# Gated attention scores counted from the middle of 128-token blocks, with six buffers of scaled keys and queries

## What is computed

```python
gcum = jnp.cumsum(gc, axis=1)                  # per key channel, within the chunk
q_t = qc * jnp.exp(gcum)                       # q was scaled by 128 ** -0.5
k_t = kc * jnp.exp(-gcum)
att = jnp.where(causal, einsum('blhk,bshk->blsh', q_t, k_t), 0.0)
o = einsum(att, vc) + einsum(q_t, state)
state = state * exp(g_end) + einsum(kc * exp(g_end - gcum), vc)
```

## Time and profile before

| | us |
|---|---|
| median of 3 runs | 1341.23 |
| the profiled execution's own time | 1341.43 |
| its span | 1339.6 |
| PE busy | 1320.0 (99%) |
| PE weight loads busy | 1119.0 (84%) |
| DVE busy | 777.4 (58%) |
| ACT busy | 641.8 (48%) |
| POOL busy | 621.8 (46%) |

### The profile page before, as it was taken

The page is one execution under the profiler, slowest core; times in us unless marked ns, Lnnn a source line. Parts: engine busy times, 40 slices in busy tenths (PEclk is TensorE's granted clock), DMA queues, the critical chain, the costliest instruction groups (busy, mean ns, idle before and its releaser), DMA issues.

```text
span 1339.6 us, 16496 instructions
## 1 busy us (share of the span) xinstructions
PE 1320.0 (99%) x6630; PEld 1119.0 (84%) x6630; DVE 777.4 (58%) x890; ACT 641.8 (48%) x1033; POOL 621.8 (46%) x294
## 2 busy tenths in 40 slices
PE   7999999999999999999999999999999999999997
PEld 6878878888898888888889888898998888888887
DVE  5857386840079998885002753386279988882002
ACT  5654787653355444443233576454554544443221
POOL 3344561245424644445553364554535544445551
PEclk9999999999999999999999999999999999999999
DMA  6332111123223332333333223301323333333331
GB/s 206 95 113 85 51 37 40 63 79 98 92 85 103 97 95 94 94 93 100 94 94 103 96 79 95 95 16 63 112 95 95 95 94 98 102 93 88 100 87 63
DMA packets 41452, 119.78 MB, mean 89 GB/s; under 512 B 4384, under 2 KB 12960, under 8 KB 41376
## 3 DMA queue, kind: packets, MB, share of 16 engines
q1 hardware_dynamic: 40160, 116.34, 28.5%
q10 hardware_dynamic: 1216, 2.38, 0.6%
HBM read 116.35 MB, written 2.23 MB: 89 GB/s over the span
## 4 chain that ended last, share of the span: by engine, by line
PE 93%; DVE 4%; ACT 1%; issue 1%; DMA 0%; ACTq 0%; DVEq 0%
PE bank L336 26%; PE bank L337 26%; PE bank L338 26%; PE bank L1774 1%; PE bank L1775 1%; PE bank L1773 1%; PE bank L2077 1%; PE bank L2059 1%; PE bank L1506 1%; PE bank L1509 1%; PE bank L1325 1%; PE bank L387 1%; PE bank L1292 1%; PE bank L1536 1%; DVE sqacc L663 1%
## 5 line engine op out<-in xcount | busy, mean ns | idle before, releaser
L319 POOL TENSOR_TENSOR wlo<-raw,whi 128x1024 fp32r<-128x1024 f32 (+2 forms) x215 | 531.1, 2483 | 633.9 <-ACT whi L313 633.8
L336 PE MATMUL bank<-xw_hi,whi 128*128 128x512 f32 (+1 forms) x1280 | 478.0, 373 | 8.6 <-DVE xw_lo L646 8.1
L338 PE MATMUL bank<-xw_hi,wlo 128*128 128x512 f32 (+1 forms) x1280 | 473.8, 370 | 0.0
L337 PE MATMUL bank<-xw_lo,whi 128*128 128x512 f32 (+1 forms) x1280 | 473.7, 370 | 0.0
L313 ACT ACTIVATE whi<-raw 128x1024 fp32r<-128x1024 f32 (+2 forms) x217 | 221.5, 1025 | 208.0 <-DMA raw<-in_fout 112.2
L336 PEld LDWEIGHTS bank<-xw_hi,whi 128*128 128x128 f32 x1280 | 242.5, 189 | 50.3 <-issue 8.9
L338 PEld LDWEIGHTS bank<-xw_hi,wlo 128*128 128x128 f32 x1280 | 242.3, 189 | 41.1
L337 PEld LDWEIGHTS bank<-xw_lo,whi 128*128 128x128 f32 x1280 | 242.5, 189 | 39.8 <-issue 0.2
L596 DVE RECIPROCAL small<-small 128x2 f32<-128x2 f32 x8 | 1.3, 165 | 315.1 <-ACT small L521 313.7
L715 DVE SCALAR_TENSOR_TENSOR cbuf<-ubuf,par,cbuf 128x510 f32<-128x510 f32 x100 | 168.7, 1687 | 3.5
L711 DVE SCALAR_TENSOR_TENSOR cbuf<-ubuf,par,cbuf 128x510 f32<-128x510 f32 x100 | 144.6, 1446 | 4.7 <-ACT cbuf L844 4.1
(11 more groups left out here) (278 smaller groups left out, 1453.9 us busy)
## 6 DMA issues: line engine op xcount, KB each, us to landing
raw<-in_fin SPq DMA_DIRECT2D x88, 512.0 KB, 3.6
raw<-in_fout SPq DMA_DIRECT2D x32, 448.0 KB, 3.3
raw<-in_gin SPq DMA_DIRECT2D x25, 512.0 KB, 3.6
raw<-in_hin SPq DMA_DIRECT2D x24, 512.0 KB, 3.7
raw<-in_hout SPq DMA_DIRECT2D x16, 512.0 KB, 3.6
raw<-in_fout SPq DMA_DIRECT2D x16, 512.0 KB, 3.6
raw<-in_gout SPq DMA_DIRECT2D x8, 512.0 KB, 3.9
xres<-in_x SPq DMA_DIRECT2D x8, 256.0 KB, 5.8
```

Of the source, the lines that this page charges most:

```text
L319: engine.tensor_tensor(wlo[s][:, 0:n], raw[s][:, 0:n], whi[s][:, 0:n].bitcast(F32), ALU.subtract).then_inc(w_lo, 1)
L336: first = nc.tensor.matmul(out_ap, wh, ah, start=start, stop=False)
L337: nc.tensor.matmul(out_ap, wh, al, start=False, stop=False)
L338: return first, nc.tensor.matmul(out_ap, wl, ah, start=False, stop=stop)
```

## The change

1. After each cumulative sum, DVE moves the origin of the exponents to the middle of each 128-token block: `dve_from_middle(t)` copies the chunk ends to `ends` (128x8) and subtracts them from every second chunk of `gl` (128x256). It is placed in turn t + 1 between `least` and the subtraction; the last one follows turn 7. With that origin one set of keys serves a whole 128-token block.
2. `dve_carries` is one add in place of 2 memsets, 8 copies and 4 adds; `carry` has one column per head, direction and request.
3. `dve_keys` is one 128x512 product in place, of `ek`; `kk`, its memsets and its 3 products by `carry` go. `qx` is `qt` times one column.
4. `scores(n)` has, for each request, three products of 128 columns (two diagonal blocks and one off it) in place of four of 64 and one of 128.
5. There are six buffers of `qt`, `ek` and `qx`. Exponents of n = 0 to 5 come after turn 7 on ACT (those of 4 and 5 behind one `hi`), keys in pairs behind the evictions of turns 9, 10 and 11 on DVE (n = 4, 5 behind the last eviction), queries one per block on POOL from block 19 on.
6. The scale 128 ** -0.5 goes into the exponent of `qt`, as a bias (ln of it). The masks are now unscaled (`up + eye` for the forward direction, `1 - up` for the backward one), and the diagonal is counted twice by the 2 that `up + eye` has on it. For d = 1, `own_scores` is one `copy_predicated` from the bank into `att` per request, in place of a product in the bank and an add.
7. On ACT the loading of the exponent table (through a 1-element `Exp`) comes behind three `cross_scores`; exponents of 4 and 5 are gone from the GLA phase; `outs(0)` is split around `cross_scores(1, 1)`.
8. Some semaphores are merged (`cst_in` and `rope_in`; the three small loads of the GLA layer; the last stores).

```diff
-                    for c in range(NCH):
-                        s = c // 2
-                        nc.tensor.matmul(out[:, s * SEQ + c * CH:s * SEQ + (c + 1) * CH],
-                                         kks(n)[:, r, c * SEQ + s * P:c * SEQ + (s + 1) * P],
-                                         qt[n % 4][:, r * SEQ + c * CH:r * SEQ + (c + 1) * CH], start=True, stop=True)
-                    c, s = (2, 0) if d == 0 else (1, 1)
-                    last = nc.tensor.matmul(out[:, s * SEQ + (1 - s) * P:s * SEQ + (2 - s) * P],
-                                            kks(n)[:, r, c * SEQ + s * P:c * SEQ + (s + 1) * P],
-                                            qx[n % 4][:, r * P:(r + 1) * P], start=True, stop=True)
+                    def against(s, queries, to):
+                        return nc.tensor.matmul(out[:, s * SEQ + to * P:s * SEQ + (to + 1) * P],
+                                                ek[n % AHEAD][:, r * SEQ + s * P:r * SEQ + (s + 1) * P], queries,
+                                                start=True, stop=True)
+                    for s in range(2):
+                        against(s, qt[n % AHEAD][:, r * SEQ + s * P:r * SEQ + (s + 1) * P], s)
+                    last = against(d, of_request(qx[n % AHEAD], r, P), 1 - d)
...
+        def dve_from_middle(dve, t):
+            d = t // GLA_HEADS
+            at, last = slice(t * NREQ * NCH, (t + 1) * NREQ * NCH), 0 if d else CH - 1
+            dve.wait_ge(sem("gate_scan"), t + 1)
+            nc.vector.tensor_copy(ends[:, at].unsqueeze(2), chunks_of(t)[:, :, last:last + 1]).then_inc(
+                sem("gate_ends"), 1)
+            dve.wait_ge(sem("gate_ends"), t + 1)
+            early = chunks_of(t)[:, d::2]
+            nc.vector.tensor_tensor(early, early, ends[:, at][:, d::2].unsqueeze(2).broadcast_to([P, NREQ * NCH // 2, CH]),
+                                    ALU.subtract).then_inc(sem("gate_mid"), 1)
...
+                    if ft:
+                        dve_from_middle(dve, t - 1)
                     dve.wait_ge(sem("gate_act"), 3 * t + 3)
...
+                if t > G0:
+                    for n in (2 * (t - G0) - 2, 2 * (t - G0) - 1):
                         dve_keys(dve, n)
...
+                if at >= BASE["gin"] + 19:
+                    pool_queries(pool, at - BASE["gin"] - 19)
...
+            nc.scalar.activation(qt[n % AHEAD][:], gl[:, f], ACT.Exp, bias=prm("lnqg"), scale=GK_NORM).then_inc(sem("gla_e"), 1)
...
+            nc.vector.tensor_tensor(ek[n % AHEAD][:], ck(gqkv, 4 + n // 2), ek[n % AHEAD][:], ALU.mult).then_inc(
+                sem("gla_kk"), 1)
...
                 if d:
-                    dve.wait_ge(sem("gla_db"), 2 * hd + 2)
                     dve.wait_ge(sem("gla_df"), 2 * hd + 2)
+                    mask = tri[:, P:2 * P].bitcast(mybir.dt.uint32).unsqueeze(1).broadcast_to([P, 2, P])
                     for r in range(NREQ):
-                        nc.vector.tensor_tensor(scores[r], scores[r], other[r], ALU.add).then_inc(sem("gla_dg"), 1)
+                        nc.vector.copy_predicated(own[r], mask, blocks(sbank(d, r)[:])).then_inc(sem("gla_db"), 1)
...
+            cross_scores(0, 0)
+            cross_scores(0, 1)
+            cross_scores(1, 0)
             nc.scalar.activation(small[:, 5:6], prm("eps"), ACT.Exp)
-            cross_scores(0, 0)
-            act_gate_exps(act, 4)
-            cross_scores(0, 1)
-            act_gate_exps(act, 5)
-            cross_scores(1, 0)
             act_gate_exps(act, 6)
-            outs(0)
+            out(0, 0)
             cross_scores(1, 1)
+            out(0, 1)
+            cross_scores(2, 0)
             act_gate_exps(act, 7)
-            cross_scores(2, 0)
             outs(1)
...
             own_scores(0, 0)
             own_scores(0, 1)
-            dve_zero_keys(dve, 3)
-            dve_keys(dve, 3)
             own_scores(1, 0)
-            dve_keys(dve, 4)
-            dve_keys(dve, 5)
+            dve_keys(dve, 6)
             own_scores(1, 1)
             own_scores(2, 0)
-            dve_keys(dve, 6)
             dve_keys(dve, 7)
...
-            for n in (4, 5):
-                pool_queries(pool, n)
             squares(0)
```

More of the change, by code:

```diff
@@ L9 @@
+import math
 from contextlib import ExitStack
@@ L33 @@
 QG = float(P) ** -0.5
+AHEAD = 6
 FF = 2816 // P
@@ L237, in build_program @@
                 tri = sb("tri", 2 * P, F32, q)
[L238 to L241, removed]
+                ek = [sb(f"ek{i}", T, F32, q) for i in range(4)] + [ek4, ek5]
+                qt = [sb(f"qt{i}", T, F32, q) for i in range(4)] + [qt4, qt5]
+                qx += [qx4, qx5]
             with ExitStack() as q:
@@ L1835, in way @@
             return ap[:, ::-1] if d else ap
-        CARRIES = 18
-        def dve_carries(dve):
[L1841 to L1867, removed]
@@ L1869, in dve_gin @@
+        def dve_carries(dve):
+            dve.wait_ge(sem("gate_ends"), G0)
+            by_chunk = ends[:].rearrange("p (i c) -> p i c", c=NCH)
+            nc.vector.tensor_tensor(carry[:].unsqueeze(2), by_chunk[:, :, 1:2], by_chunk[:, :, 2:3], ALU.add).then_inc(
+                sem("carry_set"), 1)
         def dve_gin(dve):
@@ L1995, in dve_keys @@
[L1995 to L2004, removed]
@@ L2219, in own_scores @@
                 dve.wait_ge(sem("gla_s"), 2 * hd + d + 1)
-                mask = tri[:, d * P:(d + 1) * P].unsqueeze(1).broadcast_to([P, 2, P])
-                scores = [blocks(att[hd % 2][:, r * T:(r + 1) * T]) for r in range(NREQ)]
-                other = [blocks(sbank(d, r)[:]) for r in range(NREQ)]
-                for r in range(NREQ):
-                    nc.vector.tensor_tensor((other if d else scores)[r], blocks(sbank(d, r)[:]), mask,
-                                            ALU.mult).then_inc(sem("gla_db" if d else "gla_df"), 1)
+                own = [blocks(of_request(att[hd % 2], r, T)) for r in range(NREQ)]
                 if d:
-                    dve.wait_ge(sem("gla_db"), 2 * hd + 2)
                     dve.wait_ge(sem("gla_df"), 2 * hd + 2)
+                    mask = tri[:, P:2 * P].bitcast(mybir.dt.uint32).unsqueeze(1).broadcast_to([P, 2, P])
                     for r in range(NREQ):
-                        nc.vector.tensor_tensor(scores[r], scores[r], other[r], ALU.add).then_inc(sem("gla_dg"), 1)
+                        nc.vector.copy_predicated(own[r], mask, blocks(sbank(d, r)[:])).then_inc(sem("gla_db"), 1)
+                else:
+                    mask = tri[:, 0:P].unsqueeze(1).broadcast_to([P, 2, P])
+                    for r in range(NREQ):
+                        nc.vector.tensor_tensor(own[r], blocks(sbank(d, r)[:]), mask, ALU.mult).then_inc(sem("gla_df"), 1)
             def reciprocals(hd):
```

155 lines of the change are left out of this document (54 added, 101 removed).

## The result

| | before | after |
|---|---|---|
| median of 4 runs each | 1341.33 | 1355.89 |
| the profiled execution's own time | 1341.43 | 1353.49 |
| its span | 1339.6 | 1351.7 |

The ratio after to before is 1.0106, 95% interval 1.0093 to 1.0119. The forecast was 1337.6 with a range to 1339.8. In the attention the change did what was forecast; PE had become slower ahead of it and behind it.

The account below looks back on a forecast made before the run. The prediction took PE, busy 99% of the span, as the bound. Attention gains of 4.7 us less a 1.1 us wait gave -3.6 on 1341.43, 1337.8, or 1337.6 as a median; range 1334.9 to 1339.8.

Parts of the forecast that it names:

- What costs nothing: Step listing parts priced at zero: later exponents, queries one per block, the bias and dropped scale, merged semaphores.
- PE's price of scores: Scores on PE: six weight loads replace ten at 0.111 us each, 0.445 us less per request, at most 7.1 us.
- V0 to V1: Attention, between PE's loads for the users of attention 0 and 1: 8.51 us becomes 6.35, gain 2.15.
- V1 to V2: Attention, between PE's loads for the users of attention 1 and 2: 11.25 us becomes 8.7, gain 2.55.
- V2 to V3: Attention, between PE's loads for the users of attention 2 and 3: no score in it, 5.4 us as before.
- S0 to V0: Attention's start, from the first scores to their first user on PE: PE waits 3.0 us, gain taken as 0.
- keys of 4 and 5 blocked: At the attention's start, DVE's key products wait behind POOL's instructions; without the blocking 1.9 us would be gained.
- V0 has 0.75 us to spare: First user of the attention on PE: a slower copy_predicated costs nothing there until 0.75 us is used up.
- copy_predicated: DVE's masking in the attention: taken as 0.38 us each, though no row showed this instruction.
- gate(3), +1.1: Input projection, turns 1 and 2: DVE's new product and cumulative sum are blocked by POOL, so PE waits 1.1 us.
- rival A: PE doesn't wait at gate(3), as the product or the sum gets ahead of POOL's `lo`: -4.7, 1336.5 us; chance 0.17.
- The sum without the layout: Whole kernel: -4.7 us in the attention plus 1.1 at gate(3), -3.6 us on 1341.43.

Follow-up runs that it names:

- with 512 bytes: The changed kernel with unused bytes behind the parameter tile, so everything behind stands 512 bytes further than before the change: 1336.49 us, ratio 0.9969.
- mask and add: Kernel after with 512 bytes, backward diagonal blocks masked in the bank and added instead of copy_predicated: 1338.22 us; the same on top of the later keys: 1336.34 us.
- the later keys: Kernel after with 512 bytes, keys of 4 moved behind own_scores(0, 1) and keys of 5 behind own_scores(1, 0): 1333.42 us, ratio 0.9946.
- the kernel after with 64 bytes: The changed kernel with 32 unused bytes behind the parameter tile, so tiles behind it stand 64 bytes further than before the change: 1343.12 us, ratio 1.0018.

## Why the prediction was wrong

Point by point, by its own steps:

- **The failed step** is in "What costs nothing": "The bias and the dropped scale change no instruction's size." The instructions kept their size, but the bias is read from a new column of the table, and that column moved every tile behind it by 32 bytes. The step priced it at nothing, and none of the rivals had it; the runs show 18.0 us (profiled executions of the kernel after with and without 480 bytes more). Without that shift the same change is 4.1 us faster than the kernel before.
- **PE's price of scores, V0 to V1, V1 to V2:** right. Forecast 6.35, 8.7 and 5.4 for V2 to V3; measured 6.42, 8.70, 5.41.
- **S0 to V0, keys of 4 and 5 blocked:** right in place and cause. PE waits 2.58 us (forecast 3.0), and S0 to V0 goes from 7.03 to 6.80, a gain of 0.2 (forecast 0). "V0 has 0.75 us to spare" was too much: with 512 bytes ACT's copies of S1 end at 881.63 and V0 starts at 882.20, 0.5 us to spare. DVE and POOL of the kernel after, which answer to the earlier trace rows (the rows up to 790 us are turn 1 and `least` of turn 2):
```profile
783.78 2.58 DVE L1852 TENSOR_TENSOR gl<-gl,ends 128x256 f32<-128x256 f32 x1
...
787.00 1.22 DVE L1894 TENSOR_TENSOR_SCAN gl<-gmask,ubuf 128x512 f32<-128x512 f32 x1
...
789.32 0.74 DVE L1876 TENSOR_SCALAR ubuf<-bank,par 128x512 f32<-128x512 f32 x1
...
888.88 3.17 DVE L1947 TENSOR_TENSOR ek<-gqkv,ek 128x512 f32<-128x512 f32 x2
...
892.81 0.77 DVE L2156 COPY_PREDICATED att<-tri,bank 128x256 f32<-128x256 uint32 x2
```
```profile
780.55 5.53 POOL L316 TENSOR_TENSOR wlo<-raw,whi 128x1024 fp32r<-128x1024 f32 x2 [9.25 <-ACT whi L310]
787.01 3.43 POOL L316 TENSOR_TENSOR wlo<-raw,whi 128x1024 fp32r<-128x1024 f32 x1 [0.93 <-ACT whi L310]
...
887.46 2.37 POOL L316 TENSOR_TENSOR wlo<-raw,whi 128x1024 fp32r<-128x1024 f32 x1 [1.20 <-ACT whi L310]
...
891.58 0.94 POOL L1962 TENSOR_TENSOR qx<-qt,carry 128x256 f32<-128x256 f32 x1
```
- **`copy_predicated`:** right, 0.77 for two, 0.38 to 0.39 each. That is why mask and add cost 0.76 per loop in the runs above. Whether POOL holds it up, the rows above don't show: POOL's product ends at 892.52, and it starts at 892.81. With the later keys the two overlap, and neither is longer for it:
```profile
878.74 0.78 DVE L2157 COPY_PREDICATED att<-tri,bank 128x256 f32<-128x256 uint32 x2 [0.51 <-PE bank L1990]
...
878.90 0.61 POOL L1963 TENSOR_TENSOR qx<-qt,carry 128x256 f32<-128x256 f32 x1
```
- **gate(3), +1.1:** did not come; on this point rival A held. The product was blocked as forecast (2.58 in place of 0.43 in the next turn), but the cumulative sum starts at 787.00 and POOL's `lo` at 787.01: the sum is first, takes 1.22 and not 3.3, and it is the `lo` that becomes long (3.43). `least` ends at 790.06 and gate(3) goes at 791.76 with no wait, as the products around it. The kernel after with 512 bytes has the same order (777.42 and 777.43), so the step doesn't hang on the slower pace. A margin forecast at -0.4 us came out at +0.01: the blocked product ended 0.28 us behind the `lo` that held it (786.08 to 786.36; 0.5 was assumed), and the subtraction started at 786.29, 0.07 ahead of the product's end, where 0.1 behind it was assumed.
- **The sum without the layout:** -4.7 + 1.1 was forecast, -4.87 measured in the attention. On the 1341.43 of the profile that gives 1336.6; the kernel with 512 bytes has a median of 1336.49. That is rival A's 1336.5 and not the forecast's 1337.6, though inside the range.
- **A term that was missing:** after a wait of PE of 2.6 us the clock can fall, below.

## What to carry to other kernels

An edit that adds a few bytes to a tile moves every tile behind it: before costing a change, compare where the operands of the hot loop lie, and here keep the distance of matmul's moving operand and its weights modulo 256 bytes. Where PE is busy all the time, count its instructions in a window of fixed length; the busy share hid 5 products in 135. When a change loses where none of its instructions stand, first make the old kernel with the new layout and nothing else: one run showed that no instruction of the change was to blame.

## What the runs showed of the hardware

**The distance of PE's two operands.** A product of 128x512 follows the one before after 0.2267 us, or after 0.2333 if the addresses of the activations and the weights differ from the free distance by 32 bytes; 256 and 512 are free, and a shift of both by 32 is free. It is so whichever of the two moves: in the value products of the input projection (L1769 to L1771 of the kernel after) the activations are loaded as weights and the blocks in the slots are the moving operand, and the pace is 0.233 after and 0.227 before. The Trainium skill's page "SBUF — State Buffer", section "Who interferes with whom", says that PE reads the moving operand and the weights through two ports that are independent, and that PE never waits on anyone. In this case's traces neither port has to wait for another engine as far as a row shows, but PE's pace is not independent of where the two operands lie relative to each other: 6.6 ns per product hang on their distance. That the two reads meet in the memory is a guess that no row shows.

**The clock after a wait.** Where PE had waited 2.5 to 2.7 us for the reads of S2, the granted clock fell to the 1.2 GHz level in two of four profiled executions with that wait (the kernel after with 64 bytes: 0.57 from 886 to 890 us, V0 4.23 long; the one with mask and add, above), and stayed at 1.00 in the other two. The clock there, for the kernel with 64 bytes (PE alone):
```profile
886.00:890.00 4.00, 4.00 (x18) 0.57 0.00 0
```
It cost that kernel 1.7 us: from S2 to V0 2.09 in place of 1.33, and V0, from its start to that of S3, 4.25 in place of 3.35, each against the kernel with 512 bytes. In the one with mask and add it cost 1.4 and not the 1.6 of the expectation: 1.15 in V0 and 0.25 of the 0.47 ahead of it. The other 0.2 is mask and add's own, as ACT's copies of S1 end at 882.43 and V0, which starts 0.06 behind them where it waits for them, couldn't have started before 882.49; it started at 882.74. Behind the waits of 0.2 to 1.0 us in the attention no profiled execution shows such a fall.

Whether these falls make the spread of the times isn't shown. For it: the kernel with 512 bytes spreads over 2.4 us, the one with later keys, whose wait is 0.31, over 0.9. Against it: of the ten runs with mask and add only the profiled one has a mean granted clock under 0.998, yet its 1338.82 is only 0.1 above the next. The three runs of the kernel after at 1355.87 to 1356.00, against 1353.49 profiled with the clock at 1.00, have means of 0.996 to 0.998 and stay unexplained. The mean doesn't settle it either way, since the clock also falls at the end of every version: in the kernel before it is 0.50 from 1335 us on, behind PE's last product, which a mean over a slice of the page doesn't show.

**Two engines 0.01 us apart.** Of DVE's cumulative sum at 787.00 and POOL's `lo` at 787.01 the second was held up. In turn 3 of the kernel before POOL was first, and the sum was the long one. Who begins first decides, here at a margin of 0.01 us.

**What stays open.** Why PE is slower at some distances: no row shows inside its reads, and only six distances were tried. Why at 64 the pace is 0.233 between the values of the input projection and the scores, and 0.228 in the ConvFFN. And why the clock falls after the same wait in one execution and not in another.
